# A tuned four-layer transformer kernel: layer 0's modulation rows spread by TensorE, half of the modulation products moved to GpSimd and ScalarE, four load places

## The chip, the cores and the metric

The kernel runs on one core of a Trainium2 chip. It is one launch of one hand-scheduled program, with a stream of instructions for each engine: TensorE (PE for matmuls, PEld for its weight loads), VectorE (DVE), ScalarE (ACT), GpSimd (POOL) and SyncE (SP, which here only starts loads). The metric is the device time of the launch in microseconds. Before the change it was 1287.54 us, the median of three runs (1287.22 to 1290.02).

## The reference

Two layers of one kind and two of another run over 256 tokens of width 1024. All is float32. The change touches the layers of the first kind, whose modulation is a product of one vector with a large matrix:

```python
c_act = jax.nn.silu(c)                                  # c: 1 x 1024
for l in range(DEPTH):                                  # 2 layers
    mod = c_act @ ada_w[l] + ada_b[l]                   # ada_w[l]: 1024 x 6144
    shift_m, scale_m, gate_m, shift_f, scale_f, gate_f = split(mod, 6)
    h = rms_norm(x, g_pre_mix[l]) * (1.0 + scale_m) + shift_m
    proj = h @ w_in[l] + b_in[l]                        # windowed attention on q, k, v; pooling mixer on u
    mix = concat([attn_out, pool_out]) @ w_out[l]
    x = x + gate_m * rms_norm(mix, g_post_mix[l])
    h = rms_norm(x, g_pre_ffn[l]) * (1.0 + scale_f) + shift_f
    f = (silu(h @ w_gate[l]) * (h @ w_up[l])) @ w_down[l]
    x = x + gate_f * rms_norm(f, g_post_ffn[l])
```

Then two layers of the second kind follow (latent attention, gated linear attention, retention and a convolved feed-forward part), without modulation.

## The kernel before

**Weights as a stream.** All weights lie in DRAM in the order in which they are used, cut into 233 units of at most 128 x 2048 floats (`UNITS`, L179; 1024 KB). SyncE loads them one after the other into three places of `raw_w` (`NRAW`, L30; loop at L904): unit n goes to place n % 3, and its load waits until unit n - 3 has been used up. SyncE's queue is in order, so a load that waits holds back all that follow it.

**Matmul units.** A float32 product is made of three passes. ScalarE rounds a unit into `hi_w` (`prepare`, L1030 to L1039), VectorE puts the rest into `lo_w` (`lo`, L1370 to L1379), in two halves each; `hi_w` and `lo_w` have three places. TensorE multiplies lo by hi, hi by lo and hi by hi (L474 to L476). The place in `raw_w` is free once the second half of `lo_w` is written.

**Modulation units.** The 48 units ("ada", l, n) hold two blocks each of 128 output features by 1024 inputs. VectorE multiplies each block by `c_row`, silu(c) on all partitions, and sums along the row in the same instruction (`ada`, L1381 to L1396), which gives 128 entries of `mods`, one on each partition. When the four units of a 1024-wide vector are done, `mod_column` adds bias and gain and leaves it as a column block in `modcol`.

**From column to row.** Layer 0's first shift and scale are used as columns, eight pieces at a time, while its input product runs. The other ten vectors are needed as rows, on all partitions. GpSimd's queue makes them through DRAM (`mod_row`, L961): it waits for `modcol`, writes it to `mod_rows` in 4-byte pieces (L965), waits until that has landed, and loads the row back to all 128 partitions of `rows` (L952). There are three slots in `rows`: gate, scale, shift.

**Order.** Each engine's code is written out in the order in which it runs. The table `ADA_AFTER` (L122) sets behind which matmul unit each modulation unit is loaded and multiplied: 12 of layer 0 inside its attention, 4 more and 16 of layer 1 in layer 0's feed-forward part, the last 8 in layer 1. The stages of layer 0 are: `started` (8 modulation units and the 8 input units `ink`, in four rounds j = 0 to 3), `attention_windowed(0)` with the four units `wo`, the chain of norms between mixer and feed-forward (`chain` and `ending`: square sums on ScalarE, residual and norm on VectorE, `x` times the scale row on GpSimd, transposes on TensorE; for each of the two token blocks T), then the feed-forward units `gu` (gate and up) and `wd` (down).

Of the kernel before, what the change touches and what calls it, by code (L numbers as in the profile page):

```python
# [10 lines left out]
ALU = mybir.AluOpType  # L11
# [3 lines left out]
P = 128  # L15
# [14 lines left out]
NRAW = 3  # L30
# [5 lines left out]
def const_table():  # L36
# [35 lines left out]
    diff = i[:, None] + P - k2[None, :]  # L72
    put("window", np.where((diff >= 0) & (diff < P), 0.0, NEG))
    put("causal2", np.where(diff >= 0, 0.0, NEG))
# [74 lines left out]
def unit_list():  # L149
# [9 lines left out]
    for j in range(4):  # L159
        for n in (4 + j, j):  # L160
# [103 lines left out]
def build(nc, counts, a_x, a_pos, a_const, const_at, a_vec, a_w, a_bias, a_norm, a_cnorm, a_sinks, a_gatew, a_poolw, a_c, out):  # L264
    ctx = ExitStack()
    with ctx:
# [30 lines left out]
        const = sb("const", [P, a_const.shape[1]])  # L297
# [14 lines left out]
        bias = shared[:, 0:1280]  # L312
# [5 lines left out]
        crow = sb("crow", [P, 640])  # L318
# [70 lines left out]
        def k(name, a=0, b=None):  # L389
            lo, hi = const_at[name]  # L390
# [8 lines left out]

        const_mid, const_late = const_at["window"][0], const_at["ones"][0]  # L400
# [40 lines left out]
        def _(pe):  # L441
# [114 lines left out]
            def ending(L, w, one, other, front):  # L556


                N = after(L, w)
                into_y(L, w, one, 0)  # L560
                into_y(L, w, other, 0, last=True)
                into_y(L, w, one, 1)
# [32 lines left out]
            def attention_windowed(L):  # L595
# [122 lines left out]
                for q, u in enumerate((2, 3)):  # L718
                    for T in range(2):
                        into_y(L, 0, ("wo", L, u), T, first=(q == 0))  # L720
                    attention(q)

# [179 lines left out]
        def _(sp):  # L902
            off = 0
            for n, (unit, kt, n_cols) in enumerate(UNITS):  # L904
                if unit == ("ink", 0, 2):
                    sp.dma_start(const[:, const_mid:const_late], a_const[:, const_mid:const_late]).then_inc(*sig("const_mid", 0, by=16))
                if unit == ("gu", 0, 8):
                    sp.dma_start(const[:, const_late:], a_const[:, const_late:]).then_inc(*sig("const_late", 0, by=16))
# [14 lines left out]
        def _(pool):  # L923
# [11 lines left out]
            pool.wait_ge(*due("pos_in", 0))  # L935
            pool.wait_ge(*due("const_in", 0))
            step(nc.gpsimd.tensor_copy(pos_f, pos_i))
            for T in range(2):
                step(nc.gpsimd.tensor_scalar(ang[:, 8 * T:8 * T + 8], k("freq"), pos_f[:, T:T + 1], None, ALU.mult))
            for i, quarter in ((0, 0.25), (1, 0.0)):  # L940

                step(nc.gpsimd.tensor_scalar(whole, ang, 1.0 / two_pi, quarter, ALU.mult, ALU.add))
                step(nc.gpsimd.tensor_scalar(whole, whole, magic, None, ALU.add))
                step(nc.gpsimd.tensor_scalar(whole, whole, magic, None, ALU.subtract))
                for n, c in enumerate(parts):
                    step(nc.gpsimd.tensor_scalar(part, whole, c, None, ALU.mult))
                    step(nc.gpsimd.tensor_tensor(turns[:, i, :], ang if n == 0 else turns[:, i, :], part, ALU.subtract))
                step(nc.gpsimd.tensor_scalar(turns[:, i, :], turns[:, i, :], quarter * two_pi, -3.1415925, ALU.add, ALU.max))
                nc.gpsimd.tensor_scalar(turns[:, i, :], turns[:, i, :], 3.1415925, None, ALU.min).then_inc(*sig("turns", i))
# [4 lines left out]
            pool.wait_ge(*due("ada", ("ada", 0, 7)))  # L954
            load(bias, a_bias[0:1, :], 1280, "bias_in", 0)
            pool.dma_start(sinks[:, :, :], a_sinks.rearrange("(o l) n -> o l n", o=1).to_broadcast([P, 2, HEADS])).then_inc(*sig("sinks_in", 0, by=16))
            pool.dma_start(poolw[:, :, :, :], a_poolw.rearrange("l g c d -> c l g d")).then_inc(*sig("poolw_in", 0, by=16))
# [904 lines left out]
```

## Time and profile before

| | us |
|---|---|
| median of the runs shown | 1287.54 |
| the profiled execution, its own time | 1289.59 |
| its span, first to last instruction | 1287.8 |
| PE busy | 1155.2 (90%) |
| DVE busy | 843.1 (65%) |
| ACT busy | 644.3 (50%) |
| POOL busy | 49.4 (4%) |
| mean granted TensorE clock | 0.958 |

Times in the profile are microseconds from the start of the span. An arrow names what is written and what it is written from (`lo_w<-raw_w,hi_w`). L numbers are lines of the kernel. The profiled execution ran 2.05 us longer than the median, and 1.8 us of its time lie outside the span. Busy shares are means over stages that differ much: the first 440 us hold all of the modulation, and almost all of TensorE's idle time.

### The profile page before, as it was taken

What the parts mean: (1) busy time and instruction counts of PE and PEld (TensorE: products, weight loads), DVE (VectorE), ACT (ScalarE), POOL (GpSimd) and SP (SyncE); (2) the same over time, 40 slices, a digit from 0 to 9 for tenths busy, and PEclk for the clock granted to TensorE, in tenths of its full rate; (3) what the DMA queues carried; (4) which work ended last, traced back from release to release, by engine and by line L of the source; (5) the groups of instructions that cost most, each with busy time, mean ns of one, the idle gap of its engine ahead of it and who ended that gap; (6) DMA issues with size and microseconds to landing.
All of it is one profiled execution on the core that took longest, in us unless ns stands there. A gap on an engine that the chain in (4) does not pass through costs nothing.

```text
span 1287.8 us, 19696 instructions
## 1 busy us (share of the span) xinstructions
PE 1155.2 (90%) x7883; PEld 1048.1 (81%) x7883; DVE 843.1 (65%) x1324; ACT 644.3 (50%) x1126; POOL 49.4 (4%) x73
## 2 busy tenths in 40 slices
PE   3667399997985889999999999999999999999998
PEld 2455299897975679999989888999999878999996
DVE  5788486765875766555566856755666756666654
ACT  4434263433462555434466565644556556654553
POOL 3100100000020010000000000000000000000000
PEclk9867789998997899999999999999999999999999
DMA  7859859889949526667744425555554423465551
GB/s 272 311 217 248 215 197 308 342 259 280 349 152 243 131 99 229 229 216 194 262 141 148 162 99 188 189 196 177 184 190 152 164 99 132 158 225 178 193 187 43
DMA packets 38363, 256.16 MB, mean 199 GB/s; under 512 B 4704, under 2 KB 4992, under 8 KB 9856
## 3 DMA queue, kind: packets, MB, share of 16 engines
q1 hardware_dynamic: 34416, 242.63, 56.5%
q0 software_dynamic: 3136, 10.42, 2.3%
q10 hardware_dynamic: 720, 1.84, 0.4%
q8 instruction: 63, 1.03, 0.3%
q14 instruction: 28, 0.23, 0.1%
HBM read 253.79 MB, written 1.09 MB: 198 GB/s over the span
## 4 chain that ended last, share of the span: by engine, by line
PE 63%; DMA 14%; DVE 14%; ACT 5%; issue 3%; ACTq 0%; POOL 0%; DVEq 0%; POOLq 0%
PE bank L474 20%; PE bank L476 19%; PE bank L475 19%; DMA raw_w<-weights 13%; DVE lo_w L1378 5%; DVE raw_w L1388 3%; PE bank L481 2%; ACT hi_w L1039 2%; ACT gtok L1045 1%; DMA const<-const_table 1%; PE bank L521 1%; DVE in_lo L1468 1%; DVE prob L1488 1%; DVE smax L1491 1%; PE bank L848 1%
## 5 line engine op out<-in xcount | busy, mean ns | idle before, releaser
L1378 DVE TENSOR_TENSOR lo_w<-raw_w,hi_w 128x1024 fp32r<-128x1024 f32 (+4 forms) x370 | 433.3, 1193 | 180.9 <-ACT hi_w L1039 180.2
L1039 ACT ACTIVATE hi_w<-raw_w 128x1024 fp32r<-128x1024 f32 (+4 forms) x370 | 370.6, 1027 | 259.9 <-DMA raw_w<-weights 172.6
L474 PE MATMUL bank<-in_hi,lo_w 128*128 128x256 f32 x1408 | 397.4, 282 | 5.2 <-DVE lo_w L1378 5.2
L476 PE MATMUL bank<-in_hi,hi_w 128*128 128x256 f32 x1408 | 394.0, 280 | 0.0
L475 PE MATMUL bank<-in_lo,hi_w 128*128 128x256 f32 x1408 | 394.0, 280 | 0.0
L474 PEld LDWEIGHTS bank<-in_hi,lo_w 128*128 128x128 f32 x1408 | 265.5, 189 | 8.7 <-DVE lo_w L1378 6.1
L475 PEld LDWEIGHTS bank<-in_lo,hi_w 128*128 128x128 f32 x1408 | 264.9, 188 | 1.9 <-issue 0.5
L476 PEld LDWEIGHTS bank<-in_hi,hi_w 128*128 128x128 f32 x1408 | 265.8, 189 | 0.0
L474 PE MATMUL bank<-hi_w,in_lo 128*128 128x256 f32 (+2 forms) x544 | 179.0, 329 | 33.4 <-DVE in_lo L1539 15.8
L475 PE MATMUL bank<-lo_w,in_hi 128*128 128x256 f32 (+2 forms) x544 | 174.8, 321 | 0.0
L476 PE MATMUL bank<-hi_w,in_hi 128*128 128x256 f32 (+2 forms) x544 | 174.7, 321 | 0.0
L474 PEld LDWEIGHTS bank<-hi_w,in_lo 128*128 128x128 f32 x544 | 106.6, 196 | 48.5 <-issue 21.4
L474 PE MATMUL bank<-hi_w,hid_lo 128*128 128x512 f32 x352 | 140.1, 398 | 4.3 <-DVE lo_w L1378 4.3
L475 PE MATMUL bank<-lo_w,hid_hi 128*128 128x512 f32 x352 | 139.6, 397 | 0.0
L476 PE MATMUL bank<-hi_w,hid_hi 128*128 128x512 f32 x352 | 139.4, 396 | 0.0
L1388 DVE SCALAR_TENSOR_TENSOR raw_w<-raw_w,c_row 128x1024 f32<-128x1024 f32 x96 | 113.5, 1222 | 30.0 <-DMA raw_w<-weights 21.1
L475 PEld LDWEIGHTS bank<-lo_w,in_hi 128*128 128x128 f32 x544 | 106.9, 197 | 7.3
L476 PEld LDWEIGHTS bank<-hi_w,in_hi 128*128 128x128 f32 x544 | 105.9, 195 | 8.0
L474 PEld LDWEIGHTS bank<-hi_w,hid_lo 128*128 128x128 f32 x352 | 66.5, 189 | 18.9 <-DVE lo_w L1378 4.7
L476 PEld LDWEIGHTS bank<-hi_w,hid_hi 128*128 128x128 f32 x352 | 66.5, 189 | 16.1
L475 PEld LDWEIGHTS bank<-lo_w,hid_hi 128*128 128x128 f32 x352 | 66.5, 189 | 14.4
L1299 ACT ACTIVATE shared<-bank,vcol 128x256 f32<-128x256 f32 x44 | 24.7, 562 | 98.7 <-PE bank L476 91.1
(200 smaller groups left out, 1014.1 us busy)
## 6 DMA issues: line engine op xcount, KB each, us to landing
raw_w<-weights SPq DMA_DIRECT2D x219, 1024.0 KB, 4.9
raw_w<-weights SPq DMA_DIRECT2D x8, 640.0 KB, 5.9
rows<-mod_rows POOLq DMA_DIRECT2D x10, 512.0 KB, 8.4
rows<-norm_rows POOLq DMA_DIRECT2D x5, 512.0 KB, 4.0
raw_w<-weights SPq DMA_DIRECT2D x2, 832.0 KB, 4.5
const<-const_table SPq DMA_DIRECT2D x1, 1538.0 KB, 16.9
raw_w<-weights SPq DMA_DIRECT2D x2, 768.0 KB, 4.2
shared<-bias_rows POOLq DMA_DIRECT2D x2, 640.0 KB, 10.2
```

The lines of the kernel that those rows point to most:

```text
L474: nc.tensor.matmul(o, st[1], mv[0], start=start, stop=False, **kw)
L475: nc.tensor.matmul(o, st[0], mv[1], start=False, stop=False, **kw)
L476: return nc.tensor.matmul(o, st[0], mv[0], start=False, stop=stop, **kw)
L481: last = nc.tensor.matmul(o, w, r, start=(i == 0), stop=(i == len(pairs) - 1))
L521: last = nc.tensor.transpose(b[:, P * i:P * (i + 1)], s_, k("ident"))
L848: nc.tensor.matmul(b[:, :], k(ones), head_sq[:, m, :], start=True, stop=True).then_inc(*sig("hsum", L, n))
L1039: nc.scalar.activation(hi_w[:, m % NSPLIT, cut], raw_view(unit)[:, cut], ACT.Identity).then_inc(*sig("hi_w", unit, i))
L1045: nc.scalar.activation(junk[:, :], src(c), ACT.Square, accum_out=ssq[:, T, c:c + 1]).then_inc(*sig("squared", *key, T, c))
L1299: nc.scalar.activation(conv[:, f % 2, :], ps(("gu", L, f))[:, 0:256], ACT.Identity, bias=v(f"conv_b{l}", f), scale=v(f"conv_w{l}", 44 + f) ...
L1378: nc.vector.tensor_tensor(lo_w[:, m % NSPLIT, cut], raw_view(unit)[:, cut], hi_w[:, m % NSPLIT, cut].bitcast(F32), ALU.subtract).then_inc( ...
L1388: last = nc.vector.scalar_tensor_tensor(w[:, f, :], w[:, f, :], 1.0, c_row[:, :], ALU.mult, ALU.mult, accum_out=mods[:, l, 2 * n + f:2 * n ...
L1468: nc.vector.tensor_tensor(in_lo[:, 4 * c:4 * c + 4, s_], by_tile(ps(("tr", N, T, c))[:, :]), in_hi[:, 4 * c:4 * c + 4, s_].bitcast(F32), A ...
```

## The change

- **Load places.** `raw_w` has four places instead of three. The space comes from `const` (its late part is loaded over its middle part, once layer 1's attention has used that) and from `crow`, which moves into `shared`.
- **Products on GpSimd.** 20 of the 48 modulation units (`POOL_ADA`: the first four, n = 8, 10, 16, 18, 12, 14, and every other one of layer 0's feed-forward part) are multiplied by `c_row` on GpSimd, in place, and summed by ScalarE with an activation and its accumulator (`ada_sum`). SyncE may load into such a place after the sum. In `started` the unit for GpSimd is loaded ahead of VectorE's.
- **Rows by TensorE.** Three of the ten rows, layer 0's gate 0, scale 1 and shift 1, no longer go through DRAM: TensorE multiplies `modcol`, one column broadcast to 128 x 128, by the identity into PSUM (`spread_row`, eight products for a row), and ScalarE copies two banks into `rows` (`row_in`). The other seven still go through DRAM; of these, three are now written out and read back with products of GpSimd in between.
- **Small loads.** The bias, sink, pool and gate-weight loads wait behind GpSimd's first four units; `crow` is loaded later.

```diff
-NRAW = 3
+NRAW = 4
...
+POOL_ADA = {(0, n) for n in (0, 1, 2, 3, 8, 10, 16, 18, 12, 14)} | set(_order[::2])
...
-        for n in (4 + j, j):
+        for n in (j, 4 + j):
             units.append((("ada", 0, n), *SHAPES["ada"]))
...
 # TensorE
+                if opening:
+                    banks(4, 5, 6, 7)
+                    spread_row(0, "scale", 1)
                 into_y(L, w, one, 1)
...
                     into_y(L, w, other, 1, last=True)
+                    if opening:
+                        spread_row(0, "shift", 1)
                     turn_norm(N, 0)
...
+            def spread_row(L, kind, w):
+
+                pe.wait_ge(*due("modcol", L, kind, w))
+                for c in range(2):
+                    job = ("spread", L, kind, w, c)
+                    b = take(job)
+                    for i in range(4):
+                        t = 4 * c + i
+                        last = nc.tensor.matmul(b[:, P * i:P * (i + 1)], modcol[:, ROWS[(L, kind, w)], t:t + 1].to_broadcast([P, P]), k("ident"),
+                                                start=True, stop=True)
+                    last.then_inc(*sig(*job))
...
 # SyncE
-                    sp.wait_ge(*due(*(("ada", old) if old[0] == "ada" else ("lo_w", old, 1))))
+                    sp.wait_ge(*due(*(("ada_sum" if old[1:] in POOL_ADA else "ada", old) if old[0] == "ada" else ("lo_w", old, 1))))
...
 # GpSimd
+            def products(l, n):
+
+                unit = ("ada", l, n)
+                pool.wait_ge(*due(f"raw_w{UNIT_NO[unit] % NRAW}", unit))
+                w = raw_view(unit).rearrange("p (f k) -> p f k", f=2)
+                for f in range(2):
+                    nc.gpsimd.tensor_tensor(w[:, f, :], w[:, f, :], c_row[:, :], ALU.mult).then_inc(*sig("ada_product", unit, f))
...
 # ScalarE
+            def ada_sum(l, n):
+
+                unit = ("ada", l, n)
+                w = raw_view(unit).rearrange("p (f k) -> p f k", f=2)
+                for f in range(2):
+                    sc.wait_ge(*due("ada_product", unit, f))
+                    last = nc.scalar.activation(w[:, f, :], w[:, f, :], ACT.Identity, accum_out=mods[:, l, 2 * n + f:2 * n + f + 1])
+                last.then_inc(*sig("ada_sum", unit))
...
+            def row_in(L, kind, w):
+
+                slot = ("gate", "scale", "shift").index(kind)
+                for c in range(2):
+                    copy(("spread", L, kind, w, c), rows[:, slot, cols(c)], ps(("spread", L, kind, w, c))[:, :], "row", L, kind, w, c)
...
                 for j in range(4):
                     prepare(("ink", 0, 2 * j))
+                    ada_sum(0, j)
+                    prepare(("ink", 0, 2 * j + 1))
...
                 if L == 0:
                     prepare(("wo", 0, 0))
+                    ada_sum(0, 18)
+                    ada_sum(0, 12)
                 prepare(("wo", L, 1))
...
+                if L == 0:
+                    row_in(0, "gate", 0)
+                    ada_sum(0, 14)
                 prepare(("gu", L, 0))
```

SyncE's loads in the opening, in the order of its queue, before the change (2048 columns are a modulation unit, 1280 an `ink` unit; the brackets name what is waited for):

```order
L913 DMA raw_w<-weights 128x2048 x2
L913 DMA raw_w<-weights 128x1280
L913 DMA raw_w<-weights 128x1280 [waits ada]
L913 DMA raw_w<-weights 128x2048 [waits ada]
L913 DMA raw_w<-weights 128x2048 [waits lo_w]
L906 DMA const<-const_table 128x2048
```

The same place after the change:

```order
L937 DMA raw_w<-weights 128x2048 x2
L937 DMA raw_w<-weights 128x1280 x2
L937 DMA raw_w<-weights 128x2048 [waits ada_sum]
L937 DMA raw_w<-weights 128x2048 [waits ada]
L928 DMA const<-const_table 128x1792
```

The fourth load no longer waits, and the fifth, round 1's unit for GpSimd, now waits for ScalarE's sum of round 0's; with a period of four units in `started`, all four of GpSimd's units use place 0.

ScalarE between the attention and the chain of norms in layer 0, before (L1039 `prepare`, L1151 attention outputs, L1045 square sums):

```order
L1074 ACTIVATE probT<-bank 128x512 [waits probT] x3
L1039 ACTIVATE hi_w<-raw_w 128x1024 [waits in,raw_w0]
L1039 ACTIVATE hi_w<-raw_w 128x1024
L1039 ACTIVATE hi_w<-raw_w 128x1024 [waits used,raw_w1]
L1039 ACTIVATE hi_w<-raw_w 128x1024
L1151 ACTIVATE in_hi<-bank 128x512 [waits attn] x2
L1039 ACTIVATE hi_w<-raw_w 128x1024 [waits used,raw_w2]
L1039 ACTIVATE hi_w<-raw_w 128x1024
```

And after (L1098 is `prepare`, L1138 `ada_sum`, L1242 attention outputs, L1157 into `rows` the copy in `row_in`):

```order
L1098 ACTIVATE hi_w<-raw_w 128x1024 [waits in,raw_w0]
L1098 ACTIVATE hi_w<-raw_w 128x1024
L1138 ACTIVATE raw_w,mods<-raw_w 128x1024 [waits ada_product] x4
L1098 ACTIVATE hi_w<-raw_w 128x1024 [waits used,raw_w0]
L1098 ACTIVATE hi_w<-raw_w 128x1024
L1242 ACTIVATE in_hi<-bank 128x512 [waits attn] x2
L1157 ACTIVATE rows<-bank 128x512 [waits spread] x2
L1138 ACTIVATE raw_w,mods<-raw_w 128x1024 [waits ada_product] x2
L1098 ACTIVATE hi_w<-raw_w 128x1024 [waits used,raw_w0]
L1098 ACTIVATE hi_w<-raw_w 128x1024
```

Four sums (units 18 and 12) stand ahead of the last `wo` unit's rounding, and the copies of the gate row and unit 14's sums ahead of the first `gu` unit's.

## Rows read from the trace of the kernel before

**Rows 1.** Windows: engines' busy us in a stretch, clock, DMA share, GB/s.

```profile
core 0: us, PE busy (x) PEld busy (x) DVE busy (x) ACT busy (x) POOL busy (x), PEclk, DMA share, GB/s
...
71.00:104.00 33.00, 17.83 (x84) 14.36 (x85) 30.91 (x76) 11.53 (x34) 0.91 (x1) 0.68 0.55 192
...
143.00:160.00 17.00, 0.00 (x0) 0.00 (x0) 4.88 (x6) 7.02 (x17) 3.22 (x4) 0.54 0.90 202
...
176.00:364.00 188.00, 178.47 (x1240) 166.01 (x1239) 135.44 (x196) 79.19 (x112) 4.95 (x7) 0.97 0.90 306
...
440.00:1288.00 848.00, 822.46 (x5810) 753.08 (x5808) 529.57 (x791) 462.50 (x786) 10.62 (x12) 1.00 0.49 168
```

**Rows 2.** Chain of waits, 100 to 165 us: start, us, what.

```profile
101.61 2.30 DVE raw_w L1388 x4
...
103.93 12.34 DMA raw_w<-weights
...
128.49 10.89 DMA raw_w<-weights
...
142.28 0.90 POOL mod_rows L965
...
154.56 5.33 DMA rows<-mod_rows
...
160.02 0.76 DVE normed L1447
```

**Rows 3.** Windows: two stretches after a row is written out, one without.

```profile
149.00:155.00 6.00, 0.00 (x0) 0.00 (x0) 0.95 (x2) 3.07 (x8) 0.44 (x1) 0.50 0.60 34
...
206.00:216.00 10.00, 10.00 (x64) 8.91 (x63) 3.32 (x6) 0.81 (x2) 0.56 (x1) 1.00 0.80 133
216.00:222.00 6.00, 6.00 (x52) 5.88 (x51) 4.99 (x7) 1.96 (x4) 0.00 (x0) 1.00 1.02 423
```

**Rows 4.** Chain of waits in layer 1's attention.

```profile
391.67 17.20 DMA raw_w<-weights
```

**Rows 5.** Timeline and chain of the opening: start, us, engine or what.

```profile
20.80 1.22 DVE L1388 SCALAR_TENSOR_TENSOR raw_w<-raw_w,c_row 128x1024 f32<-128x1024 f32 x1
...
21.88 1.35 ACT L1039 ACTIVATE hi_w<-raw_w 128x640 fp32r<-128x640 f32 x2
...
55.96 1.22 DVE L1388 SCALAR_TENSOR_TENSOR raw_w<-raw_w,c_row 128x1024 f32<-128x1024 f32 x1
...
57.22 10.04 DMA raw_w<-weights
...
70.73 0.61 DVE tok L1549
```

**Rows 6.** Groups by form: count, busy us, mean ns, idle before.

```profile
L1039 ACT ACTIVATE hi_w<-raw_w 128x1024 fp32r<-128x1024 f32 x342 | 351.2, 1051 | 237.5 <-DMA raw_w<-weights 150.2 <-PE bank L476 87.1
...
L1074 ACT ACTIVATE in_hi<-bank 128x512 fp32r<-128x512 f32 x28 | 16.3, 597 | 21.3 <-PE bank L521 20.8
...
L1378 DVE TENSOR_TENSOR lo_w<-raw_w,hi_w 128x1024 fp32r<-128x1024 f32 x342 | 411.1, 1223 | 178.3 <-ACT hi_w L1039 177.8
```

**Rows 7.** The page's DMA issues: count, KB each, us to landing.

```profile
raw_w<-weights SPq DMA_DIRECT2D x219, 1024.0 KB, 4.9
```

**Rows 8.** Timelines of POOL and DVE where both read SBUF.

```profile
19.67 1.21 DVE L1388 SCALAR_TENSOR_TENSOR raw_w<-raw_w,c_row 128x1024 f32<-128x1024 f32 x1
...
19.93 1.01 POOL L942 TENSOR_SCALAR start<-start 128x16 f32<-128x16 f32 x1
...
22.22 0.26 POOL L944 TENSOR_SCALAR start<-start 128x16 f32<-128x16 f32 x1
...
155.14 2.49 POOL L983 TENSOR_TENSOR scaled<-x,rows 128x512 f32<-128x512 f32 x2
167.57 2.99 POOL L983 TENSOR_TENSOR scaled<-x,rows 128x512 f32<-128x512 f32 x2 [9.95 <-DVE x L1431]
...
169.84 1.93 DVE L1447 SCALAR_TENSOR_TENSOR normed<-scaled,tok_rstd,rows 128x512 f32<-128x512 f32 x2 [1.69 <-ACT tok_rstd L1054]
```

More of the change, by code:

```diff
@@ L311, in build @@
         shared = sb("shared", [P, 1536])
-        bias = shared[:, 0:1280]
+        bias, crow = shared[:, 0:1280], shared[:, 0:640]
         gates = shared[:, 0:1024].rearrange("p (t s) -> p t s", t=4)
@@ L978, in scale @@
                         pool.wait_ge(*due("x", L, w, T, c))
-                        if T == 0 and c == 0:
-                            pool.wait_ge(*due("row1", N[1], "scale", 0 if N[0] == "mix" else 1))
+                        if T == 0:
+                            row = (N[1], "scale", 0 if N[0] == "mix" else 1)
+                            if row != (0, "scale", 1):
+                                pool.wait_ge(*due("row1", *row))
+                            else:
+                                pool.wait_ge(*due("row", *row, c))
                         if T == 1:
@@ L984, in scale @@
                             *sig("scaled", N, T, c))
-            mod_row(0, "gate", 0)
-            mod_row(0, "scale", 1)
-            mod_row(0, "shift", 1)
+            pool.wait_ge(*due("c_act", 0))
+            products(0, 0)
+            angles()
+            for n in range(1, 4):
+                products(0, n)
+            load(bias, a_bias[0:1, :], 1280, "bias_in", 0)
+            pool.dma_start(sinks[:, :, :], a_sinks.rearrange("(o l) n -> o l n", o=1).to_broadcast([P, 2, HEADS])).then_inc(*sig("sinks_in", 0, by=16))
+            pool.dma_start(poolw[:, :, :, :], a_poolw.rearrange("l g c d -> c l g d")).then_inc(*sig("poolw_in", 0, by=16))
+            pool.dma_start(gatew[:, :, :], a_gatew.rearrange("l g n -> g l n")).then_inc(*sig("gatew_in", 0, by=16))
+            for n in (8, 10, 16, 18, 12, 14):
+                products(0, n)
+            pool.wait_ge(*due("tok", 0, 1, 2))
+            load(bias, a_bias[1:2, :], 1280, "bias_in", 1)
             scale(("ffn", 0), 0, 0)
             pool.wait_ge(*due("normed", ("ffn", 0), 1, 1))
-            mod_row(0, "gate", 1)
-            pool.wait_ge(*due("scaled", ("ffn", 0), 1, 1))
-            mod_row(1, "scale", 0)
-            mod_row(1, "shift", 0)
-            pool.wait_ge(*due("tok", 0, 1, 2))
-            load(bias, a_bias[1:2, :], 1280, "bias_in", 1)
+            products(0, 20)
+            products(0, 22)
+            row_out(0, "gate", 1)
+            products(1, 0)
+            products(1, 2)
+            row_back(0, "gate", 1)
+            row_out(1, "shift", 0)
+            products(1, 4)
+            products(1, 6)
+            row_back(1, "shift", 0)
+            row_out(1, "scale", 0)
+            products(1, 8)
+            products(1, 10)
+            row_back(1, "scale", 0)
+            products(1, 16)
+            products(1, 18)
             scale(("mix", 1), 0, 1)
@@ L1000, in _ @@
             mod_row(1, "gate", 0)
-            pool.wait_ge(*due("scaled", ("mix", 1), 1, 1))
             mod_row(1, "scale", 1)
@@ L1366, in in_turn @@
             def in_turn(unit):
+                while UNITS[taken[0]][0][0] == "ada" and UNITS[taken[0]][0][1:] in POOL_ADA:
+                    taken[0] += 1
                 assert UNITS[taken[0]][0] == unit, (unit, UNITS[taken[0]][0])
@@ L1391, in ada @@
                 if n % 4 == 3 and not (l == 0 and n < 8):
-                    ve.wait_ge(*due("ada", unit))
+                    for m in range(n - 3, n + 1):
+                        ve.wait_ge(*due("ada_sum" if (l, m) in POOL_ADA else "ada", ("ada", l, m)))
                     g = n // 4
@@ L1419, in residual @@
                     return
-                ve.wait_ge(*due("row0", L, "gate", w))
+                if (L, w) != (0, 0):
+                    ve.wait_ge(*due("row0", L, "gate", w))
                 for c in range(2):
+                    if (L, w) == (0, 0):
+                        ve.wait_ge(*due("row", 0, "gate", 0, c))
                     job = ("y", L, w, T, c)
```

111 lines of the change are left out of this document (66 added, 45 removed).

## Prediction, made before the changed kernel was run

> **What bounds the kernel now.** I read the windows by stage first [rows 1]. From 440 us on TensorE is busy for 822.46 of 848 us: nothing done to modulation reaches far in there. In layer 0's feed-forward part (176 to 364) it is busy for 178.47 of 188 us. The idle time lies ahead: from 71 to 104 us TensorE works 17.83 of 33 us, while VectorE works 30.91, and from 143 to 160 it does not work at all, at a granted clock of 0.54. So the change must be priced on the path through the first 176 us, and after that only against small gaps.
>
> The chain of waits says what that path is [rows 2]. Up to 104 us it is VectorE's own work, modulation products among it (101.61, 2.30 us for a unit's two halves). Then come waits for weights of 12.34 and 10.89 us, though a plain unit lands in a median of 4.9 us [rows 7]. Then a row is written out (142.28) and read back (154.56, 5.33 us to landing), and only then can VectorE make `normed` at 160.02.
>
> The windows tell why those landings are long [rows 3]. Behind a row that is written in 4-byte pieces the core moves 34 GB/s (149 to 155) and 133 GB/s (206 to 216), while right after the latter it moves 423. Ten rows do this. One in layer 1's attention makes a wait of 17.20 us [rows 4].
>
> **The change part by part.** I follow two marks of layer 0: the first bias add of its attention (70.73 before) and the first `normed` of its feed-forward norm (160.02 before).
>
> *Opening, up to the first mark.* Before, round 0's products end at 22.0 (20.80 + 1.22) and round 3's at 57.2 (55.96 + 1.22) [rows 5], 11.7 us for a round. Now the sum of round 0 stands on ScalarE behind the rounding that ends at 23.2 (21.88 + 1.35) and takes two activations of 1.05 us [rows 5, 6], 2.2 with what the accumulator takes: 25.4, so +3.4. After that each round is a closed loop through place 0, because SyncE's queue is in order and the next unit for GpSimd goes where the last one was: landing 4.9 [rows 7], product, sum 2.2. The trace has no product of 128x1024 on GpSimd; two of 128x512 take 2.49 us together with VectorE idle [rows 8], so I take 2.4 for a half and 4.9 for a unit, between 4.6 (some of the 1.24 is fixed) and 5.0. The loop is 12.0 us with nothing in its way. One wait for VectorE in each product (1.2, below) and, in round 1, a rounding that waits for an `ink` unit behind the constants make it 13.8: the last sum is at 25.4 + 41.4 = 66.8, +9.6. The `wo` unit behind it then waits for landing as before (10.04 [rows 5]), with 0.3 MB less beside it: mark 1 at +9. Ends: +4 with 12.0 us a round, +14 when every half also loses 1.2 us and ScalarE is late in each round.
>
> *The shared path of GpSimd and VectorE.* A GpSimd instruction of 0.26 us takes 1.01 us when it starts inside a VectorE product that reads two tensors in SBUF, and ends right behind it; GpSimd's pair of 2.49 us takes 2.99 when it starts inside VectorE's `x` (167.57); and VectorE's pair of `normed` takes 1.93 us for two of 0.76 when GpSimd's runs (169.84) [rows 8]. So the one that comes later waits for the whole of the other. Each of the 40 products can therefore hold VectorE for up to 2.4 us, 96 us in all, where VectorE is relieved of 20 x 2.4 = 48. Work that VectorE reads from PSUM is not shown to wait.
>
> The Trainium skill has a rule that speaks against this change: in "SBUF — State Buffer", section "Who interferes with whom", the port pair that VectorE and GpSimd share is an exclusive lock, held for the whole instruction, and a VectorE instruction with two SBUF inputs contends with a GpSimd one that reads SBUF. By that rule, the trace agrees, moving a product is no relief for VectorE wherever it has two-input work waiting; a rule of shared bandwidth would have stretched both a little, and the sum would then go by the lower ends below.
>
> *Attention, 71 to 104 us.* Units 8, 10 and 16 leave VectorE. Unit 8's products fell into a wait for TensorE's bank, so two units count: -4.8. ScalarE's sum of unit 10 stands ahead of a `wo` rounding: +1.3. Six GpSimd halves run here, 14.4 us; the softmax reads PSUM and reduces one tensor, so I let 2.5 us reach VectorE (ends 0 and 14). Together -1, between -4.8 and +10.6.
>
> *104 to 160 us.* No row is written out here any more. The two landings lose what exceeds 4.9: 7.4 + 6.0 us. The round trip from 142.28 to 160.02 is 17.7 us; ScalarE's 7.0 us of the norm chain inside it [rows 1] stay, and so does one copy of 0.6 [rows 6]: 10.1 us go. That is -23.5. Unit 18 off VectorE: -2.4. Units 12 and 14 are needed last, and on the path each now takes product and sum, 4.9 + 2.2, in place of 2.4: +4.7 twice. The gate and scale rows' four copies of 0.6 [rows 6] stand ahead of ScalarE's chain: +2.4. TensorE's spreading is 24 products of 128 columns in its idle time: 0, and if they are late they are part of these. Together -14; ends -19 (one of units 12 and 14 covered) and -7 (half of the other six halves' 14.4 us held against VectorE). Late next is ScalarE: rounding, sum and copies in one queue. Mark 2 comes at 9 - 1 - 14 = -6.
>
> *Feed-forward of layer 0.* 53 units in 188 us, 10.5 turns of two `gu`, one `wd`, two modulation units. VectorE's 135.44 us [rows 1] are 12.9 a turn; one unit less and GpSimd's 4.9 in its way, 15.4, against 17.0 of TensorE (178.47 / 10.5). It fits, narrowly. TensorE's idle 9.5 us are all that can be gained; three rows are still written out here, with one more place ahead. I take -3, between -9.5 and +9 (in 10 turns one `lo_w` half of 1.22 [rows 6] reaches TensorE, less the 3). GpSimd's later `scaled` products wait behind its own only if it is late, which 4.9 of 17 us a turn does not make it.
>
> *Layer 1's attention.* The long wait [rows 4] has 12.3 us over a plain landing. One place more issues a load one unit earlier, about 3 us at that pace: -3, between -12.3 and 0. Its three rows stay. *After 440 us:* 25.5 us of idle spread thin, and loads that land in time: 0 (from -3 to +2). The moved `crow`, bias and constant loads: 0, they have tens of us, but if the bias loads are late they hold mark 1, which the +14 has.
>
> *Sum:* -6 - 3 - 3 = -12 on the span of 1287.8, 1275.8; with the 1.8 us outside it 1277.6 for a profiled execution. The one before ran 2.05 over the median, so the median comes to about 1275.5; I say 1276.
>
> **The rivals.**
>
> *More gain.* GpSimd's products fall where VectorE waits or reads PSUM. For it: VectorE is idle 35% of the whole. Then +4, -4.8, -18.6, -6, -3: -28, 1259. Against it: in 71 to 104 us VectorE has 2 idle us of 33.
>
> *Nothing left.* The fourth place is eaten: a GpSimd unit holds its place for 4.9 + 2.1 (a rounding ahead of the sum) + 2.2 = 9.2 us where VectorE's held it for 2.4, and SyncE's queue stops behind it. With 4.9 for landing that is 14.1 us for four places, 3.5 a unit, against 188 / 53 = 3.5 now. Then feed-forward is +4, layer 1 0: 1286.
>
> *Slower.* The lock, in one mechanism: GpSimd holds the shared path when VectorE's `lo_w` is due, and TensorE waits for `lo_w`. My sum lets about 12 of the 96 us reach the path; from about 24 on the change loses, and with a third of them, 34, it is +22 on the forecast: 1298. For it: the rows of the exclusive wait, and that `lo_w` reads two SBUF tensors. Against it: three places of split weights ahead of TensorE.
>
> **How the numbers follow.** The forecast (1267 to 1285 by itself) 0.55, more gain 0.17, nothing left 0.10, slower 0.18. The range takes in half of each outer case: 1257 to 1294. A difference of 0.2%, 2.6 us, is what a measurement of this kernel can tell. Faster by more: 0.53 + 0.17 + 0.04 = 0.74; within: 0.07; slower 0.19.
>
> **What would show it.** The chain should no longer hold `rows<-mod_rows` ahead of the first feed-forward norm, and TensorE's gap there should shrink from 17 us and more to about 8. The first `tok` add should come near 80 us; if it is at 71, my loop through place 0 is wrong. `normed` near 154. GpSimd's products should take 2.4 us alone and up to 3.6 against VectorE, and some `lo_w` over 3 us. PE busy in the feed-forward window should stay near 178. A `tok` add after 85 us, or a feed-forward part longer than 190 us, would make the forecast wrong, and so would a `normed` before 145.

## Result and the profile after

The changed kernel takes 1291.74 us (median of 14 runs, 1286.07 to 1296.96), the one before 1287.3 us (median of 14 beside them). The ratio is 1.0032, with a 95% interval of 1.0016 to 1.0047: slower by 0.3%, where -11.5 us had been forecast. The profiled execution has a span of 1291.5 us, 3.7 more than before.

The stretches of [rows 1], in the windows of the changed kernel (same columns):

```profile
71.00:104.00 33.00, 16.16 (x82) 12.45 (x82) 26.19 (x46) 8.82 (x20) 10.11 (x4) 0.76 0.57 221
143.00:160.00 17.00, 17.00 (x107) 14.32 (x106) 11.04 (x16) 7.56 (x12) 6.77 (x3) 1.00 0.90 357
176.00:364.00 188.00, 181.17 (x1277) 169.81 (x1276) 140.32 (x160) 103.31 (x159) 61.51 (x28) 0.97 0.86 295
440.00:1288.00 848.00, 826.08 (x5815) 756.74 (x5813) 528.58 (x791) 463.78 (x793) 11.18 (x13) 0.99 0.49 169
```

In the third stretch VectorE has 36 instructions fewer than before (160 for 196) and is busy for 140.32 us in place of 135.44. Fewer instructions and more time: that is the line to see first.

The chain of waits from 79 us to the norm ahead of the feed-forward part (start, us, what), which answers to [rows 2] and to the last two rows of [rows 5]:

```profile
68.63 7.75 DMA raw_w<-weights
...
79.86 0.61 DVE tok L1655
...
80.50 1.71 DVE tmp L1665
...
106.15 5.87 DVE lo_w L1476 x2
...
122.00 6.58 DVE raw_w L1486 x4
...
142.55 9.00 DMA raw_w<-weights
151.62 6.23 POOL raw_w L982 x2
...
168.10 0.76 DVE normed L1553
```

The round trip of the row is gone, and so is the landing of 12.34 us. In their place stand VectorE's own pieces at more than twice their length: two `lo_w` halves alone take 2.36 us (77.50 below) and here 5.87; a unit's two products took 2.30 [rows 2] and here 6.58. The last row but one is GpSimd's unit 14 at 6.23 us: the chain to the norm runs through it, though TensorE still has work beside it (busy 17.00 of 17 us from 143 to 160). The norm comes at 168.10, where 154 was forecast and 160.02 was before.

The timelines of POOL and VectorE show who holds whom (start, us, engine, line, operation; [rows 8] before). In the attention:

```profile
77.50 2.36 DVE L1476 TENSOR_TENSOR lo_w<-raw_w,hi_w 128x1024 fp32r<-128x1024 f32 x2 [4.05 <-ACT hi_w L1098]
...
78.94 10.11 POOL L982 TENSOR_TENSOR raw_w<-raw_w,c_row 128x1024 f32<-128x1024 f32 x4 [11.63 <-DMA raw_w<-weights]
...
80.50 1.71 DVE L1665 TENSOR_TENSOR tmp<-tok,rope 128x128 f32<-128x128 f32 x1
82.14 2.42 DVE L1666 TENSOR_TENSOR tmp<-tok,rope 128x128 f32<-128x128 f32 x1
84.59 2.25 DVE L1667 TENSOR_TENSOR tok<-tmp 128x64 f32<-128x64 f32 x1
86.76 2.37 DVE L1668 TENSOR_TENSOR tok<-tmp 128x64 f32<-128x64 f32 x1
```

Four rotary operations: the first waits for the rest of the half that GpSimd is running, each of the others for a whole one. In the kernel without GpSimd's products (below) the same operations take 0.29, 0.28, 0.22 and 0.22 us. In the feed-forward part:

```profile
196.32 4.97 POOL L982 TENSOR_TENSOR raw_w<-raw_w,c_row 128x1024 f32<-128x1024 f32 x2 [9.75 <-DMA raw_w<-weights]
...
196.53 2.48 DVE L1887 TENSOR_TENSOR hid_lo<-hidden,hid_hi 128x256 fp32r<-128x256 f32 x1 [0.48 <-ACT hid_hi L1401]
198.94 0.41 DVE L1882 TENSOR_TENSOR hidden<-silu,bank 128x256 f32<-128x256 f32 x1
199.27 3.11 DVE L1476 TENSOR_TENSOR lo_w<-raw_w,hi_w 128x1024 fp32r<-128x1024 f32 x1
```

`hid_lo` (0.41 us alone) is held until the first half ends. `hidden`, which reads one operand from PSUM, runs beside the second half at its usual 0.41. `lo_w` is held to that half's end at 201.29 and then takes its own 1.1.

The groups by form (count, busy us, mean ns, idle before), [rows 6] before:

```profile
L1476 DVE TENSOR_TENSOR lo_w<-raw_w,hi_w 128x1024 fp32r<-128x1024 f32 x342 | 441.0, 1310 | 177.0 <-ACT hi_w L1098 176.3
L982 POOL TENSOR_TENSOR raw_w<-raw_w,c_row 128x1024 f32<-128x1024 f32 x40 | 107.7, 2712 | 181.3 <-DMA raw_w<-weights 171.8 <-ACT c_row L1087 8.2 <-DVE normed L1553 1.3
L1486 DVE SCALAR_TENSOR_TENSOR raw_w<-raw_w,c_row 128x1024 f32<-128x1024 f32 x56 | 76.9, 1409 | 22.6 <-DMA raw_w<-weights 22.6
```

Over 342 `lo_w` the mean rose from 1223 ns [rows 6] to 1310, 30 us; over VectorE's 56 products it is 187 ns above the 1222 of a free one, 10 us. GpSimd is held as well: the shortest of its 40 halves took 2330 ns, the mean is 2712. Of 1024 KB loads the median landing is 4.9 us, as in [rows 7]. The long wait of layer 1's attention [rows 4] is still there:

```profile
402.60 16.66 DMA raw_w<-weights
```

And where gate 1's row is written out now (209.93), the windows show the slow transfer of [rows 3] again, a little later:

```profile
211.00:217.00 6.00, 6.00 (x52) 5.91 (x51) 4.05 (x5) 2.98 (x5) 0.00 (x0) 1.00 1.30 327
217.00:223.00 6.00, 6.00 (x31) 5.00 (x30) 0.42 (x1) 0.11 (x1) 4.24 (x2) 1.00 0.82 117
```

### The profile page after: what moved, and what is told of

It is laid out like the page before. It is cut to its first block, busy times and chain, and to the rows that moved or that the text cites. A ratio compares the mean times of both kernels' runs of the same rounds, so it can differ in the third digit from the quotient of the medians.

```text
span 1291.5 us, 19860 instructions
## 1 busy us (share of the span) xinstructions
PE 1162.4 (90%) x7931; PEld 1056.2 (82%) x7931; DVE 850.8 (66%) x1244; ACT 688.9 (53%) x1212; POOL 149.7 (12%) x107
## 3 DMA queue, kind: packets, MB, share of 16 engines
q10 hardware_dynamic: 720, 1.97, 0.4%
## 4 chain that ended last, share of the span: by engine, by line
PE 65%; DVE 13%; DMA 8%; ACT 6%; issue 3%; POOL 0%; DVEq 0%; ACTq 0%
PE bank L476 21%; PE bank L478 20%; PE bank L477 20%; DMA raw_w<-weights 8%; DVE lo_w L1476 5%; PE bank L483 2%; ACT gtok L1104 1%; DVE raw_w L1486 1%; ACT hi_w L1098 1%; ACT raw_w L1138 1%; PE bank L523 1%; DVE in_lo L1574 1%; DVE prob L1594 1%; DVE smax L1597 1%; PE bank L870 1%
## 5 line engine op out<-in xcount | busy, mean ns | idle before, releaser
L1476 DVE TENSOR_TENSOR lo_w<-raw_w,hi_w 128x1024 fp32r<-128x1024 f32 (+4 forms) x370 | 467.5, 1285 | 177.1 <-ACT hi_w L1098 176.3
L1098 ACT ACTIVATE hi_w<-raw_w 128x1024 fp32r<-128x1024 f32 (+4 forms) x370 | 370.5, 1026 | 198.6 <-DMA raw_w<-weights 107.2
L982 POOL TENSOR_TENSOR raw_w<-raw_w,c_row 128x1024 f32<-128x1024 f32 x40 | 107.7, 2712 | 181.3 <-DMA raw_w<-weights 171.8
L1486 DVE SCALAR_TENSOR_TENSOR raw_w<-raw_w,c_row 128x1024 f32<-128x1024 f32 x56 | 76.9, 1409 | 22.6 <-DMA raw_w<-weights 22.6
```

What stands on the lines that cost most here:

```text
L982: nc.gpsimd.tensor_tensor(w[:, f, :], w[:, f, :], c_row[:, :], ALU.mult).then_inc(*sig("ada_product", unit, f))
L1098: nc.scalar.activation(hi_w[:, m % NSPLIT, cut], raw_view(unit)[:, cut], ACT.Identity).then_inc(*sig("hi_w", unit, i))
L1476: nc.vector.tensor_tensor(lo_w[:, m % NSPLIT, cut], raw_view(unit)[:, cut], hi_w[:, m % NSPLIT, cut].bitcast(F32), ALU.subtract).then_inc( ...
L1486: last = nc.vector.scalar_tensor_tensor(w[:, f, :], w[:, f, :], 1.0, c_row[:, :], ALU.mult, ALU.mult, accum_out=mods[:, l, 2 * n + f:2 * n ...
```

## Experiments

Every ratio is against the kernel before, timed beside it on the same chip. The letters L, C, S, Q, R, D and B in the expectations name rival explanations and are explained there. The first four experiments take the change apart.

**All products on VectorE.** Four places and three rows by TensorE stay; GpSimd multiplies nothing.

```diff
-POOL_ADA = {(0, n) for n in (0, 1, 2, 3, 8, 10, 16, 18, 12, 14)} | set(_order[::2])
+POOL_ADA = {(0, n) for n in ()}
...
-        for n in (j, 4 + j):
+        for n in (4 + j, j):
```

The edit also puts VectorE's `ada(0, n)`, the order of ScalarE's roundings in the opening and the wait ahead of the small loads back to what they were, or nearly so: in the opening it changes more than who multiplies.

> The whole change without GpSimd's products and ScalarE's sums: four places and the three rows by TensorE, all 48 modulation units multiplied and summed on VectorE in the order of the kernel before. L: both gains and no lock, 1265 to 1270, faster than either part alone. If VectorE itself were the bound, as a reason for the move would have it: above 1275. R: no better than places_only.

Measured: 1251.37 us, 0.9693 (0.9673 to 0.9712). Without GpSimd's part the rest of the change is worth 3.07%, 39.6 us, more than any theory on record had for it.

**Rows alone** (in addition `NRAW = 3`) and **places alone** (four places, all ten rows through DRAM):

> Three rows of layer 0 by TensorE, but three load places and every modulation product on VectorE as before (the constants' layout, crow and the small loads as in the change). Theory L (GpSimd's products block VectorE on the shared path, and that ate what the rows gave): the rows are worth what the landings and the round trip lost, about 15 us, so 1287 - 15 = 1272, and the first feed-forward norm comes near 146 instead of 160. Rival R (the rows through DRAM were hidden anyway, something else ends at the same time): within 3 us of 1287.

> Four load places, all ten rows through DRAM and every product on VectorE as before. L: the places are worth little by themselves in layer 0, where VectorE and the rows set the pace, and about 3 us in layer 1's attention and 2 in the feed-forward part: 1282. Rival Q (what ate the gain is that places are held too long and SyncE's queue stops): with nobody holding them, four places give 10 us or more, 1277.

Measured: 1276.48 us, 0.9890 (0.9871 to 0.9909), and 1265.11 us, 0.9803 (0.9783 to 0.9824). 1.10% and 1.97% add up to the 3.07% of both. The rows came as expected (`normed` at 146.9 us); the places gave 25 us where I had expected 5, and rival Q 10 or more. In the windows from one norm to the next (of the kernel before, of places alone), TensorE goes from 12.2 us of idle time to 2.0 and from 195.82 busy to 190.99, at a granted clock of 0.98 for 0.96:

```profile
160.00:368.00 208.00, 195.82 (x1339) 181.77 (x1340) 151.59 (x215) 93.32 (x144) 9.86 (x11) 0.96 0.84 287
```

```profile
154.00:347.00 193.00, 190.99 (x1339) 178.65 (x1340) 151.10 (x215) 93.50 (x144) 9.37 (x10) 0.98 0.86 297
```

The places gain at both kinds of time. From 170 to 343 us TensorE has no idle time left (173.0 busy of 173), so all of the 9.5 idle us inside my window of [rows 1] went, and 0.6 more at the stage's start. The busy time fell by 4.8 us. Before, TensorE waited in the middle of the stage at a granted clock below full; with four places the same part runs without a wait at 1.00 (before, then places alone):

```profile
290.00:302.00 12.00, 8.41 (x48) 8.20 (x48) 4.64 (x7) 1.58 (x2) 1.10 (x2) 0.72 1.06 169
```

```profile
176.00:330.00 154.00, 154.00 (x1100) 144.15 (x1100) 122.48 (x179) 67.05 (x94) 4.42 (x6) 1.00 0.96 328
```

With the rows alone, all that is left between 83 and 150 us of the three landings that held the chain before (12.34, 6.28 and 10.89 us) is one of 4.67:

```profile
132.97 4.67 DMA raw_w<-weights
```

VectorE's own products are the costliest line on that chain now (18.9% of it, 10.9% between 100 and 165 us before), and TensorE's three passes make another 21% of it. So the stretch gains 13 us and not the 23.5 that I had counted.

**No read on GpSimd.** The changed kernel with each product replaced by two memsets of the same block, so that GpSimd still occupies itself and holds its places.

```diff
-                    nc.gpsimd.tensor_tensor(w[:, f, :], w[:, f, :], c_row[:, :], ALU.mult).then_inc(*sig("ada_product", unit, f))
+                    step(nc.gpsimd.memset(w[:, f, :], 0.0))
+                    nc.gpsimd.memset(w[:, f, :], 0.0).then_inc(*sig("ada_product", unit, f))
```

> The changed kernel, but each of GpSimd's products is replaced by two fills of the same block, one after the other, which read nothing in SBUF; the modulation products are left out by it. Waits, load places, ScalarE's sums and their order stay. L: VectorE is no longer held (lo_w back to 1.22 us each, 0 instead of 57 us of excess), and if a fill takes about as long as half a product the total falls from 1292 by a third to a half of 57: 1270. Q (ScalarE's sums and the held places are the cost): 1288 to 1292.

Measured: 1264.41 us, 0.9785 (0.9765 to 0.9805). From the changed kernel that is 2.47%, 32 us, back; 1270 us had been expected. This kernel leaves the modulation products out, and two memsets hold GpSimd for 1.9 us where a product holds it for 2.3, so it changes the length too; the short products below separate the two. From layer 1's attention on, where GpSimd has no product, it takes as long as the changed kernel (919.6 and 919.3 us), so the other values that it computes with did not show in the time. `lo_w` is at its free length again although GpSimd writes beside it (group by form, then the two timelines, POOL and VectorE):

```profile
L1477 DVE TENSOR_TENSOR lo_w<-raw_w,hi_w 128x1024 fp32r<-128x1024 f32 x342 | 411.0, 1222 | 187.9 <-ACT hi_w L1099 187.3
```

```profile
188.55 0.95 POOL L982 MEMSET raw_w<- 128x1024 f32 x1 [4.55 <-DMA raw_w<-weights]
189.55 0.95 POOL L983 MEMSET raw_w<- 128x1024 f32 x1
...
188.52 1.23 DVE L1477 TENSOR_TENSOR lo_w<-raw_w,hi_w 128x1024 fp32r<-128x1024 f32 x1 [0.53 <-ACT hi_w L1099]
189.99 1.22 DVE L1477 TENSOR_TENSOR lo_w<-raw_w,hi_w 128x1024 fp32r<-128x1024 f32 x1
```

A page's rule states both halves of this: the Trainium skill, "SBUF — State Buffer", section "Who interferes with whom", has a VectorE instruction with two SBUF inputs contend with a GpSimd one that reads SBUF, "not with one that only writes it". The trace agrees, with 1222 ns beside memsets and 1310 beside products.

**GpSimd's products in one stage only.** From the kernel with all products on VectorE: GpSimd takes the first four units; or the six of the attention; or every other one of the feed-forward part.

```diff
+POOL_ADA = {(0, n) for n in (0, 1, 2, 3, )}
...
+POOL_ADA = {(0, n) for n in (8, 10, 16, 18, 12, 14, )}
...
+POOL_ADA = {(0, n) for n in ()} | set(_order[::2])
```

> Four places and rows by TensorE, GpSimd's products only for the first four units; the other 44 on VectorE. The traces of the changed kernel and of the one with every product on VectorE put the first bias add at 79.8 and 63.6 us, with VectorE held for only 8 us there. Theory C (a closed loop through place 0: landing, product, sum, next load) says that these four units cost the whole difference: 1251 + 16 = 1267. Theory L (only the lock): 1251 + 8 = 1259 at most.

> The same, with GpSimd's products only for the six units in layer 0's attention (8, 10, 16, 18, 12, 14). L: between the marks the changed kernel takes 88.3 us and the one with all on VectorE 72.8, of which the kernel whose GpSimd only fills keeps nothing (66.8): 1251 + 15 = 1266. If the six cost only because the opening had put the loads out of step: 1251 to 1256.

> The same, with GpSimd's products only for every other one of the 20 units of layer 0's feed-forward part. My prediction held that it fits there narrowly (15.4 of 17.0 us a turn). L and the held places: the feed-forward part goes from 193 to about 204 us: 1251 + 10 = 1261. If it fits: 1251 or less.

Measured: 0.9816 (0.9792 to 0.9840), 0.9827 (0.9806 to 0.9849) and 0.9784 (0.9757 to 0.9810): +1.23%, +1.34% and +0.91% over all products on VectorE, 3.48% together, where all three at once cost 3.39%, 43.7 us. All three came near what L or C had said. None of the three pays. The first keeps the changed kernel's order of loads and roundings in the opening, so its 1.23% is the price of both together. Each costs its time in its own stage, which the marks of the profiled executions show (us: first `tok` add, from there to the first `normed` of the feed-forward norm, from there to the next mixer's `normed`, the rest):

| kernel | to `tok` | to `normed` | feed-forward 0 | rest |
|---|---|---|---|---|
| before | 70.7 | 89.3 | 208.3 | 919.5 |
| after | 79.8 | 88.3 | 204.1 | 919.3 |
| rows alone | 70.7 | 76.1 | 207.1 | 920.0 |
| places alone | 64.7 | 88.8 | 193.8 | 919.2 |
| all on VectorE | 63.6 | 72.7 | 193.3 | 920.5 |
| no read | 76.7 | 66.8 | 199.5 | 919.6 |
| opening | 78.1 | 73.9 | 196.0 | 919.1 |
| attention | 64.3 | 87.8 | 193.8 | 917.8 |
| feed-forward | 65.1 | 72.7 | 207.3 | 920.4 |

Each line is one execution. That of "feed-forward" ran 5.6 us over its kernel's median, those of "opening" and "places alone" 3.2 over, that of "attention" 1.9 under, so a few us of a line can be its execution's own.

With the reads gone, the relief of VectorE in the attention shows: 66.8 us in "no read" for 72.7 with all products on VectorE. The late start is not the reason, since a kernel that also starts late (75.3) but has these products on VectorE takes 72.9 (the short products in the opening, next). The idea of the change was worth about 6 us there, and the lock cost more than three times that.

**What holds place 0 in the opening.** The opening costs 14.5 us up to the first `tok`, and "no read" gives back only 3 of these. I had put it down to the length of product and sum in a closed loop, so the products were cut to a sixteenth, in the opening alone and in the whole changed kernel.

```diff
-                    nc.gpsimd.tensor_tensor(w[:, f, :], w[:, f, :], c_row[:, :], ALU.mult).then_inc(*sig("ada_product", unit, f))
+                    nc.gpsimd.tensor_tensor(w[:, f, 0:64], w[:, f, 0:64], c_row[:, 0:64], ALU.mult).then_inc(*sig("ada_product", unit, f))
```

> All four places, three rows by TensorE, and GpSimd's products for the first four units only, but each product instruction takes 64 of the 1024 columns (so most of these four units' product is left out, and ScalarE's sum runs over data not multiplied). The waits, the order of the units and ScalarE's sums stay. The same kernel with whole products was 1.23% slower than with all products on VectorE (ratio 0.9816 against 0.9693; first tok at 78.1 us of the span against 63.6). Theory L (the time goes to VectorE's instructions held up by the running products): in the stretch before the first tok VectorE lost at most a few us that way, so by L alone the first tok falls by 3 or 4 us to 74 to 75, ratio near 0.979. Theory C (a closed loop through place 0: the next load into it waits for product, then sum, and all loads behind it in SP's queue wait with it): 4.4 us less in each of four turns, first tok at 62 to 67, ratio 0.970 to 0.974. Theory S (what holds the place is the sum's turn in ScalarE's queue, behind the rounding of the weights, and not the product): first tok stays at 76 to 79 and the ratio at 0.980 to 0.982.

> The changed kernel with each of its forty GpSimd products cut to 64 of 1024 columns (most of the product of twenty modulation units is left out; the sums on ScalarE run over whole blocks, the waits and the order stay). The changed kernel was at 1.0032, the one with memsets in place of the products (3.9 us a unit, no lock) at 0.9785, the one with all products on VectorE at 0.9693. Theory L plus C: the lock is gone as with the memsets, and the 3.4 us a unit that the memsets still took go too, so 0.970 to 0.974. Theory L with Q (what is left beside the lock is ScalarE's sums and the queues, not the products' length): 0.977 to 0.980, as with the memsets. If VectorE's relief (20 units of 2.3 us that it no longer multiplies) were worth something once lock and length are gone, the ratio falls below 0.969.

Measured: 0.9820 (0.9782 to 0.9858) with the first `tok` at 75.3, and 0.9785 (0.9751 to 0.9819). Theory C fell: fifteen sixteenths of the products' length gave back 2.8 us of 14.5. L had said 74 to 75 and S 76 to 79, so 75.3 does not part these two.

The second kernel is also the control that "no read" needs. Its GpSimd instructions read both tensors but are short, and it measures the same 0.9785; the stretch from `tok` to `normed` takes 67.5 us and `lo_w` is at its free length:

```profile
L1476 DVE TENSOR_TENSOR lo_w<-raw_w,hi_w 128x1024 fp32r<-128x1024 f32 x342 | 411.7, 1224 | 182.7 <-ACT hi_w L1098 182.1
```

So the loss goes when GpSimd does not read, and also when it reads only for a short time. From 3.9 us a unit (memsets) down to 0.6 (short products, not held up) nothing more is gained: that GpSimd holds a place longer is not what the 32 us are made of.

The timeline of ScalarE in the changed kernel shows what holds place 0. Unit 0's products end at 13.3 us of the span, and its sum runs at 24.05, behind four copies of the turned input and a rounding:

```profile
21.70 1.20 ACT L1157 ACTIVATE raw<-bank 128x512 f32<-128x512 f32 x2 [0.34 <-PE bank L523]
22.80 1.35 ACT L1098 ACTIVATE hi_w<-raw_w 128x640 fp32r<-128x640 f32 x2
24.05 1.05 ACT L1138 ACTIVATE raw_w<-raw_w 128x1024 f32<-128x1024 f32 x1
```

**The sum earlier in ScalarE's queue**, with whole products in the opening only: first ahead of its turn's rounding, then unit 0's at the head of the queue as well.

```diff
+                    ada_sum(0, j)
                     prepare(("ink", 0, 2 * j))
-                    ada_sum(0, j)
```

The second kernel has, in place of the added line:

```diff
+                ada_sum(0, 0)
...
+                    if j > 0:
+                        ada_sum(0, j)
```

> GpSimd's products, whole, for the first four units only, as in the kernel that measured 0.9816 with its first tok at 78.1 us, with one change: ScalarE's sum of unit j now stands ahead of the rounding of the input weights of the same turn, and not behind it. With the products cut to a sixteenth that kernel still had its first tok at 75.3, so the products' length is not what holds place 0. Theory S (the place is held because the sum waits in ScalarE's queue behind a rounding whose weights land later): in the first turn the sum now ends near 27 us in place of 37 (absolute time), and the loads of the next turns start 9 us and then a few us earlier; first tok at 66 to 70, ratio 0.972 to 0.975. Theory D (the order of the loads, modulation unit j before 4 + j, or the contention of loads sets it, whatever ScalarE does): first tok stays at 76 to 79, ratio 0.980 to 0.983.

> As the kernel with the sums moved ahead of the rounding (0.9792, first tok at 72.8 us), and the first unit's sum moved further, to the head of ScalarE's queue, before the sums of squares of x. In that kernel the first products ended at 23.6 us (absolute time), the sum ran at 33.3, since ScalarE's four copies of the turned input stood ahead of it, and the next load into place 0 was issued at 35.5; with all products on VectorE the corresponding load went out at 21.4. Theory S (ScalarE's queue holds the place): the load goes out near 26, the second turn's modulation units land some 8 us earlier, the first tok comes at 64 to 69, ratio 0.972 to 0.977. Theory B (ScalarE's waiting for the product delays the input's norm by about as much as the place is freed earlier): first tok at 71 to 75, ratio 0.978 to 0.983.

Measured: 0.9792 (0.9767 to 0.9816), first `tok` at 72.8, between what S and D had said; and 0.9739 (0.9714 to 0.9763), first `tok` at 71.2, where B had put it (71 to 75), but with the ratio in S's range. Both moves together take back 0.77% of the opening's 1.23%; the first `tok` came forward by 6.9 us of 14.5. SyncE's queue shows the fifth load going out at 14.51 us in place of 26.25 (first the changed kernel, then the sum at the head):

```profile
26.25 0.80 SPq L937 DMA_DIRECT2D raw_w<-weights  x2
```

```profile
14.51 1.39 SPq L937 DMA_DIRECT2D raw_w<-weights  x2
```

With the sum out of the way the product is on the chain to the first `tok`, which in the last round it was not in the changed kernel (a rounding and the sum, 66.53 us, stood in its place). The chain with the sum ahead of the rounding:

```profile
47.84 6.67 DMA raw_w<-weights
...
54.58 5.27 POOL raw_w L984 x2
...
61.05 8.36 DMA raw_w<-weights
```

So my loop of landing, product and sum is real, but comes second, behind ScalarE's queue. With all products on VectorE the chain does not run through a weights load there at all: it ends in the small load of `sinks` (9.67 us from 53.81). How much of the rest the changed order of the loads (theory D) makes was not tested by itself.

**Three more rows by TensorE** (layer 1's gate 0, scale 1 and shift 1), all products on VectorE:

```diff
-                opening = (L, w) == (0, 0)
+                opening = L < 2 and w == 0
```

> The kernel with every product on VectorE, four places, and now also layer 1's gate 0, scale 1 and shift 1 by TensorE: six of ten rows no longer go through DRAM. If a row through DRAM costs what its slow loads cost others (three in layer 0 gave 14 us of 1290), these three, which fall into layer 1's attention with a wait of 17 us for weights before the change, give 5 to 10: 1243. If what waits there is covered by the fourth place: 1249 to 1251.

Measured: 1248.52 us, 0.9680 (0.9660 to 0.9701), against 0.9693 for three rows: the intervals overlap, so the second three rows gave nothing clear of the noise, and 1243 us, the gain that I had thought possible, did not come. It is the fastest kernel of the study, 3.2% under the one before and 3.5% under the changed one (0.9680 / 1.0032).

## Why the prediction was wrong

The forecast was 12 us faster; it came out 4 slower. Two of its terms were far too small, with opposite signs, and the small error of the sum hides both. That 1291.7 us lies inside my range of 1257 to 1294 is no merit of the sum: the range took in half of the slower rival.

- **Opening, +9: right in size, partly for another reason.** The first `tok` came at 79.8 (+9.1). It is the sum of two things: four places alone bring it 6 to 7 us forward (64.7 and 63.6), and GpSimd's units, with the order of loads and roundings that came with them, put it back by 14.5. I had named the closed loop through place 0, but made it of product, sum and landing. The runs show that the products' length in it is worth 2.8 us (78.1 to 75.3 with a sixteenth of them), and the sum's place in ScalarE's queue 6.9 (78.1 to 71.2).
- **The step that failed: "so I let 2.5 us reach VectorE".** From the first `tok` to `normed` I had -15 and measured -1.0. Taking the lock away makes the same stretch 66.8 us ("no read") or 67.5 (short products) in place of 88.3: the lock costs about 21 us there, where I had let 2.5. The other terms of that stretch were off too, but by less: I had counted 3.5 us of cost for moving its units apart from the lock (-4.8 and -2.4 for VectorE's relief, +1.3 and +9.4 for sums and products on the path), and 72.7 to 66.8 is a gain of 5.9. My reason for 2.5, that the softmax reads PSUM, held for those rows; but GpSimd's halves met the rotary operations, `lo_w` and VectorE's own products, which all read two tensors in SBUF. I had the rule, the row that showed it, and the 14.4 us of GpSimd's halves, and then took a value near the lower end without looking at what VectorE had to do when each unit would land.
- **The lock in all.** Of the 96 us that I had as its most, 32 reached the path, which is the third that the slower rival named (it wrote 34). My sum said that it let 12, but the terms in it that name the lock make only 6: 1.2 in each of three rounds, and 2.5 in the attention. As a mechanism the rival is the right one; it said 1298 for 1291.7, with the other terms mis-sized as in my own sum. What speaks against it, three places of split weights ahead of TensorE, did not cover the lock; why not was not tested.
- **Four places: a part of two terms of -3, and nothing in the opening.** The runs show 1.97%, 25 us; in the profiled execution 6 of them are in the opening and 14.5 in the feed-forward part. There I took 3 us of the 9.5 that TensorE sat idle, and wrote that these were all that could be gained. All 9.5 went, and 4.8 us more came from busy time at a higher granted clock (0.98 for 0.96), which I had put at nothing. By the clocks alone, 195.8 x 0.96 / 0.98, I estimate 4.0 of these 4.8. Layer 1's attention took 97.3 us from norm to norm in the changed kernel for 99.7 before (-2.4, where I had -3), and 98.5 with places alone; only with three more rows by TensorE did it fall to 94.1.
- **Rows by TensorE: 23.5 - 2.4 counted, 13 measured** (76.1 for 89.3). The waits did go; VectorE's own products and TensorE's passes were late next, and I had not priced what stood behind the waits.
- **Feed-forward, -3: measured -4.2, by luck.** It is -15 for the places and +11 for GpSimd (all on VectorE 193.3, after 204.1). "It fits, narrowly" was wrong: it set VectorE's sum of 15.4 us against TensorE's 17.0 and left out that a short operation waits for a whole product. That "nothing left" was near in its total (1286) is luck of the same kind.
- **After 440 us, 0:** near. The rest is 919.3 us for 919.5, but with layer 1's attention in it, which gave 2.4; what follows that took 2.2 us more than before, a little over my upper end of +2.

What the loss on GpSimd's side is made of: 43.7 us, of which 32 go with the reads of SBUF. The table splits the 12 that are left (0.92%): "no read" against all on VectorE is +13.1 in the opening, -5.9 to the norm, +6.2 in the feed-forward part and -0.9 behind. In the opening the sum's place in ScalarE's queue was shown (0.77%, though measured without the other stages' products). The 6.2 us are not resolved: with short products the feed-forward part took 194.6. Nor is it resolved why it took 198.6 us with the sum at the head, where no product of GpSimd runs, and 193.3 with all products on VectorE; that execution ran 3.1 us over its kernel's median, at a granted clock of 0.967 for 0.974 to 0.976 in the other three.

## What to carry to other kernels

Before elementwise work goes to GpSimd, list what VectorE will run while it is there, by operand: each two-input SBUF operation of 0.2 us can wait for a whole 2.4 us instruction. The price of a collision is the rest of the other engine's instruction, not what the waiting one moves: with GpSimd's instructions cut to 0.3 us the mean of `lo_w` was 1224 ns for 1310. Whether the whole product in many short instructions would pay was not tried. Take a change with several parts apart before judging it: here two good parts (3.1%) and one bad one (3.4%) added up to "no change". When a queue's place is freed by another engine, look at where the freeing instruction stands in that engine's queue, not only at how long it takes.

## What the runs showed of the hardware

- A GpSimd product of 128x1024 takes 2.33 us when nothing holds it, one of 128x64 0.31 (the shortest of 40 in each case). From these two I estimate 2.1 ns a column and 0.2 us whatever the size. The mean of the 40 short ones is 0.59 us, because some of them are held by VectorE's instructions and take up to 1.38. A memset of 128x1024 takes 0.95 us.
- VectorE and GpSimd alternated, one instruction each, for eight instructions in a row (78.94 to 89.13 us): neither engine got ahead, and operations of 0.22 to 0.29 us took up to 2.42.
- With the fourth load place the feed-forward stage of layer 0 ran at a mean granted clock of 0.98 in place of 0.96, and TensorE's busy time for the same matmuls was 4.8 us less: closing 10.2 us of waits (12.2 to 2.0) shortened the stage by 14.5. In the stretch where TensorE had waited most (3.6 of 12 us, from 290) the granted clock had been 0.72.
